# Feed-forward down products: seven products of quarters in place of eight, in all chunks but each stage's first, with the gated units' hidden tiles cut 6, 8, 8

## The reference, cut to what matters

```python
# two MLP stages, i = 0, 1 (D_FF = 4096)
u = jnp.square(jax.nn.relu(h @ mlp_w1[i])) @ mlp_w2[i]
h = _layer_norm(DN_ALPHA * h + u, ln2_g[i], ln2_b[i])
...
# four gated stages (D_FF_2 = 2816), layers l = 0, 1, before and after a mixer
def _swiglu(x, w_gate, w_up, w_down):
    return (jax.nn.silu(x @ w_gate) * (x @ w_up)) @ w_down
x = x + MACARON * _swiglu(_rmsnorm(x, ffn1_norm), ffn1_w_gate, ffn1_w_up, ffn1_w_down)
```

## Time and profile before

| | |
|---|---|
| device time, median of 3 runs | 3332.48 us (3332.04 to 3334.54) |
| span of the profiled execution, first to last instruction | 3327.9 us |
| outside the span, against the median | 4.6 us |
| PE busy | 3224.8 us, 97% |
| DVE busy | 2011.6 us, 60% |
| ACT busy | 1456.2 us, 44% |
| POOL busy | 872.9 us, 26% |

### The profile page before, as it was taken

One profiled execution on the slowest core, in us unless ns is written; L12 is line 12 of the kernel. 1 busy time (PEld: TensorE's weight loads), 2 busy tenths in 40 slices (PEclk: granted clock), 3 DMA queues, 4 the chain that ended last, 5 costly groups with the idle time before them and its releaser, 6 DMA issues.

```text
span 3327.9 us, 47776 instructions
## 1 busy us (share of the span) xinstructions
PE 3224.8 (97%) x20089; PEld 2867.4 (86%) x20092; DVE 2011.6 (60%) x3009; ACT 1456.2 (44%) x2244; POOL 872.9 (26%) x401
## 2 busy tenths in 40 slices
PE   8999999999999999999999999999999999999998
PEld 6887889988668899888999788999999998789998
DVE  6568755445866544576747636574766476367646
ACT  4465445443534544454434324453454343235433
POOL 3210033321400233303232430323222323312232
PEclk9999999999999999999999999999999999999999
DMA  4310233331102333323222322332332323223332
GB/s 133 105 50 26 99 98 112 101 119 58 64 26 89 102 114 102 109 71 125 92 85 97 114 81 84 115 102 83 115 102 89 103 83 125 76 89 108 96 96 76
DMA packets 239814, 308.97 MB, mean 93 GB/s; under 512 B 8336, under 2 KB 168096, under 8 KB 239088
## 3 DMA queue, kind: packets, MB, share of 16 engines
q1 hardware_dynamic: 236016, 291.41, 26.8%
q0 software_dynamic: 3584, 14.52, 1.2%
HBM read 303.80 MB, written 2.10 MB: 92 GB/s over the span
## 4 chain that ended last, share of the span: by engine, by line
PE 78%; DVE 16%; ACT 4%; issue 2%; DMA 0%; POOL 0%; DVEq 0%; ACTq 0%; POOLq 0%
PE bank L598 24%; PE bank L600 24%; PE bank L599 24%; DVE wlo L2082 3%; ACT whi L1322 2%; PE bank L979 1%; DVE wraw L2104 1%; DVE xl L2155 1%; PE bank L618 1%; DVE raw_w L2104 1%; PE bank L1261 1%; PE bank L1252 1%; PE bank L1186 0%; DVE st L2113 0%; DVE wkk_o L2899 0%
## 5 line engine op out<-in xcount | busy, mean ns | idle before, releaser
L3140 POOL TENSOR_TENSOR wlo<-wraw,whi 128x1024 fp32r<-128x1024 f32 (+2 forms) x209 | 531.1, 2545 | 1374.3 <-ACT whi L1322 1374.1
L598 PE MATMUL bank<-xh,whi 128*128 128x256 f32 (+1 forms) x2456 | 721.0, 294 | 46.4 <-DVE zt L2277 17.9
L1322 ACT ACTIVATE whi<-wraw 128x1024 fp32r<-128x1024 f32 (+3 forms) x426 | 441.1, 1039 | 678.7 <-PE bank L600 546.2
L600 PE MATMUL bank<-xh,wlo 128*128 128x256 f32 (+1 forms) x2456 | 715.7, 291 | 0.0
L599 PE MATMUL bank<-xl,whi 128*128 128x256 f32 (+1 forms) x2456 | 711.8, 290 | 0.0
L3140 POOL TENSOR_TENSOR wlo<-raw_w,whi 128x1024 fp32r<-128x1024 f32 (+1 forms) x126 | 300.6, 2389 | 867.4 <-ACT whi L1322 867.4
L598 PEld LDWEIGHTS bank<-xh,whi 128*128 128x128 f32 x2456 | 464.5, 189 | 66.8 <-issue 27.1
L598 PE MATMUL bank<-whi,uh_w 128*128 128x512 f32 x1216 | 473.9, 390 | 0.0
L600 PE MATMUL bank<-whi,ul_w 128*128 128x512 f32 x1216 | 473.3, 389 | 0.0
L599 PEld LDWEIGHTS bank<-xl,whi 128*128 128x128 f32 x2456 | 464.5, 189 | 10.2
L599 PE MATMUL bank<-wlo,uh_w 128*128 128x512 f32 x1216 | 473.2, 389 | 0.0
(11 more groups left out here) (392 smaller groups left out, 5009.7 us busy)
## 6 DMA issues: line engine op xcount, KB each, us to landing
wraw<-in_w_in SPq DMA_DIRECT2D x26, 1024.0 KB, 5.1
wraw<-in_ffn_w_down SPq DMA_DIRECT2D x20, 1024.0 KB, 5.0
raw_w<-in_ffn_w_down SPq DMA_DIRECT2D x20, 1024.0 KB, 5.1
raw_w<-in_mlp_w SPq DMA_DIRECT2D x19, 1024.0 KB, 5.1
wraw<-in_mlp_w SPq DMA_DIRECT2D x17, 1024.0 KB, 5.3
wraw<-in_ffn_w_gate SPq DMA_DIRECT2D x32, 512.0 KB, 4.6
raw_w<-in_ffn_w_gate SPq DMA_DIRECT2D x32, 512.0 KB, 4.8
raw_w<-in_ffn_w_up SPq DMA_DIRECT2D x32, 512.0 KB, 4.4
```

What stands on the lines that cost most here:

```text
L598: M.matmul(o, lh, rh, start=start, stop=False, skip_group_check=more)
L600: return M.matmul(o, ll, rh, start=False, stop=stop, skip_group_check=more)
L1322: A.activation(hi, raw, ACT.Copy).then_inc(*k.w_hi.inc(("hi", j)))
L3140: G.tensor_tensor(lo[:, 0:n], raw[:, 0:n], hi[:, 0:n].bitcast(F), ALU.subtract).then_inc(*k.w_lo.inc(("lo", j)))
```

## The change

The down product of every chunk but a stage's first is now done by the same scheme of seven products. The two operands are u (two halves of 256 tokens by two halves of 4 hidden tiles) and the down weights of the chunk (two halves of 4 hidden tiles by two halves of 512 columns). The planner's new `grid` writes 14 items for such a chunk (seven products, each in two parts of 2 hidden tiles, called a and b here, as in 5a and 5b); an item is now 2 token tiles x 2 hidden tiles x 3 = 12 matmuls of 128x512. The order of issue is 1, 2, 5, 6, 3, 7, 4.

- TensorE: 168 matmuls of 128x512 for a chunk in place of 192 (`grid` in the tensor program). Products 1, 6, 7 share one bank for each token tile, as do 5 and 3; a later product of such a chain adds to what stands in the bank, after VectorE has read it.
- ScalarE: 14 high parts of weights of 1024 columns (before 8), and the seven high parts of u's operands with 1024 columns (`u_high`) in place of eight with 512.
- VectorE: four sums of u quarters (`u_sum`, for 7, 6, 5 and 3), seven low parts of u's operands with 1024 columns (`u_low`) in place of eight with 512, eight sums of weight quarters (5, 6, 7 and 4, two parts each), three low parts of weights (3a, 3b, 4b; `ON_DVE`), and 16 additions of a bank to `h` (`add`) in place of 8.
- GpSimd: 11 low parts of weights (before 8).
- Gated stages are cut 6, 8, 8 (`GLU_PARTS`) instead of 8, 8, 6, so the chunk of 6 is the plain first one. All up units of a gated stage now have four tiles.
- The down weights arrive as four loads of 4 tiles x 512 columns, each filling a raw slot until the last of its products has been split.
- The load of `pT` stands in the MLP's first chunk instead of its last, into another buffer; the reserved DMA scratch is set to 8192 bytes.

The diff, cut to its core: the tables and the planner, TensorE's new `grid`, then the MLP's rows in the scalar program (`high_u`, `u_high`) and in the vector program (`u_sum`).

```diff
+GLU_PARTS = ((0, 6), (6, 14), (14, 22))
+GRID = (1, 2, 5, 6, 3, 7, 4)
+CHAIN = {1: "a", 6: "a", 7: "a", 5: "b", 3: "b", 2: "c", 4: "d"}
+HOST = {1: "11", 2: "21", 3: "22", 4: "21", 5: "11", 6: "11", 7: "12"}
+ADDS = {1: ((0, 0),), 2: ((0, 0),), 5: ((1, 1),), 6: ((0, 1),), 3: ((0, 1),), 7: ((1, 1), (1, 0)), 4: ((1, 0),)}
+ON_DVE = ((3, 0), (3, 1), (4, 1))
...
+    def grid(self, tag, key, view):
+
+        u, pair = Unit(key, 0, 0), self.pairs(4)
+        for n, (name, k, c) in enumerate((("11", 0, 0), ("21", 4, 0), ("12", 0, 512), ("22", 4, 512))):
+            u.loads[name] = self.load(view[:, k:k + 4, c:c + 512], [2 * pair[n], 2 * pair[n] + 1])
+            self.loads[u.loads[name]].name, self.loads[u.loads[name]].unit = name, u
+        for p in GRID:
+            u.items[p] = [self.item(tag, u.loads[HOST[p]], 1, 2 * part, 2 * part + 2, "dve" if (p, part) in ON_DVE else "pool", u, p, part)
+                          for part in range(2)]
...
+    def grid(u, last, turn_after):
+
+        tail = 0
+        for p in GRID:
+            key = [("grid", u.key, CHAIN[p], t) for t in range(2)]
+            uh, ul = k.wide.u[p]
+            for part in range(2):
+                j = slots.get("down")
+                wh, wl = weights(j)
+                pe.wait_ge(at("u operand", u.key, p))
+                for t in range(2):
+                    if part == 0 and p in (1, 5, 2, 4):
+                        take(key[t], True)
+                    elif part == 0:
+                        pe.wait_ge(at("added", u.key, {6: 1, 7: 6, 3: 5}[p], t))
...
+            def high_u(n, p):
+                if q and (n, p) in ((1, 1), (1, 5), (1, 4)):
+                    u_high(d, {1: 1, 5: 7, 4: 2}[p], at("u used", "up", i, q - 1))
...
+                u_high(d, 5, at("u used", "up", i, q - 1))
+                grid(d, last, 2, between=high_p if last else None)
...
+                u_sum(d, 6)
+                u_sum(d, 5)
+                grid(d, 1.0, last, 2, between=low_p if last else None)
```

More of the change, by code:

```diff
@@ L261, in load, with item @@
         return len(self.loads) - 1
-    def item(self, tag, load, n, k0, kn, low, unit=None, p=None):
+    def item(self, tag, load, n, k0, kn, low, unit=None, p=None, part=0):
         if n == 2:
@@ L268, in item @@
         before = sorted({self.split_at[x] for x in halves if x in self.split_at})
-        self.items.append(Item(tag, self.loads[load], halves, before, k0, kn, low, unit, p))
+        self.items.append(Item(tag, self.loads[load], halves, before, k0, kn, low, unit, p, part))
         for x in halves:
@@ L1036, in glu @@
         s = k.wide
-        parts = chunks(DFF2 // 128)
+        parts = GLU_PARTS
         g = 2 * l + which
@@ new lines, in u_low, with grid @@
+    def u_low(d, p):
+        hi, lo = k.wide.u[p]
+        dve.wait_ge(at("u high", d.key, p))
+        V.tensor_tensor(lo, k.wide.u32[p], hi.bitcast(F), ALU.subtract).then_inc(*done.inc(("u operand", d.key, p)))
+    def grid(u, scale_y, last, turn_after, stage=None, between=None):
+        tail = 0
+        for p in GRID:
+            for part in range(2):
+                slots.get("down")
+                slots.done()
+                if part == 0 and p in (1, 2, 5, 6):
+                    if p == 2:
+                        u_sum(u, 3)
+                    u_low(u, {1: 5, 2: 6, 5: 3, 6: 4}[p])
+                if part == 0 and p == 3 and between:
+                    between()
+                if part:
+                    add(u, p, scale_y, last, stage)
+                if last and p in (7, 4) and tail < 3:
+                    if tail == turn_after:
+                        ho.finish(1)
+                        ho.turn(0)
+                    if tail == min(turn_after + 1, 2):
+                        ho.turn(1)
+                    if tail >= turn_after:
+                        slots.prepare()
+                    tail += 1
@@ new lines, in add @@
+    def add(u, p, scale_y, last, stage):
+        for n, (th, ch) in enumerate(ADDS[p]):
+            for t in range(2):
+                tt, c, key = 2 * th + t, 512 * ch, ("grid", u.key, CHAIN[p], t)
+                x = h[:, tt, c:c + 512]
+                dve.wait_ge(at("product", u.key, p, t))
+                if p in (2, 3, 7, 4):
+                    dve.wait_ge(at("added to", u.key, {2: 1, 3: 6, 7: 5, 4: 7}[p], t) if n == 0 else None)
+                names = [("added to", u.key, p, t)]
+                if n == len(ADDS[p]) - 1:
+                    names.append(("added", u.key, p, t))
+                    if p in (2, 3, 7, 4):
+                        names.append(("free", key))
+                ends = last and ENDS.get(p) == (th, ch)
+                if ends:
+                    names.append(("h", ho.round, tt, c))
+                V.scalar_tensor_tensor(x, ring.of(key)[:, :], scale_y, x, ALU.mult, ALU.add).then_inc(*done.inc(*names))
+                if ends:
+                    if stage and p == 4 and t:
+                        barrier(stage)
+                    ho.updated(tt, c, p in (3, 4))
```

336 lines of the change are left out of this document (235 added, 101 removed).

## The result

The changed kernel takes 3492.66 us (median, 3490.93 to 3495.71), the kernel before 3332.26 in the same comparison: a ratio of 1.0481, 95% interval 1.0466 to 1.0496. It is 160 us slower. The forecast was 3442 with a range to 3495, so the sign and the range held, and the size was 51 us short. The result lies 2 us inside the range's upper end, and outside the stretch of 3400 to 3465 to which the prediction gave its best chance.

A forecast was written before the change was run, and what follows sets the result against it. TensorE's matmul count bounds the kernel now; in quarters, VectorE and GpSimd excluding each other on SBUF would. Six MLP chunks +55 and four gated stages +54, together +109 on 3332.5, gave 3442 us, range 3345 to 3495.

The forecast's parts named there:

- the lock: Down product in quarters: VectorE instructions with two SBUF inputs and GpSimd low parts exclude each other; 45.3 us against 38.3 of matmuls.
- walk: Queue-by-queue timing of a quarter down product: 52.9 us in an MLP, 50.5 in a gated stage, against 43.7 before.
- first mark 11.65: MLP down product: GpSimd has item 2b's low part ready at 11.65 us after TensorE's first matmul, due at 8.2.
- the handover at the end of a stage: Last down product of a stage (45.5 against 43.7 us): left as it is, bounds 0 and 2 us for each of six.
- locked instructions: VectorE instructions with both inputs in SBUF, which exclude a GpSimd low part for their whole length; taken at 1.18 us each.
- so it gives nothing back: Up product behind an MLP's quarter down product: 37.9 us of VectorE and GpSimd taking turns in 39.7, costed at no change.
- bound from above: Raw slots of down weights held until 7b is split at 42.7 us; queued loads cost 0 to 3 us a chunk, up to 40.
- a gain of under 1 us a stage: Gated stages' up units with four tiles instead of two: same matmuls, half the instructions per tile, costed at nothing.
- the forecast's span of 3437: Whole kernel: +109 us on the profile's own 3327.9 us; the same +109 on 3332.5 gives the forecast time 3442.
- the clock rival: TensorE's waits in quarter chunks also drop its clock, 1.7 us a fall, 24 or 48 us in all: 3466 to 3490, chance 0.15.
- 20 us fewer on GpSimd: Argument against the faster rival: up products run without a stall because they have 20 us fewer on GpSimd than quarter down products.
- The fast rival: Quarter down products: supply keeps up, stalls stay under 5.5 us a chunk; 3281, or 3256 with the remaining queue hidden; chance 0.13.

## Why the prediction was right in sign and short in size

**Right: the lock is the bound of a down product in quarters.** The walk's 52.9 and 50.5 us were 50.2 and 48.0, its first mark 11.65 was 11.56, its waits were ended by GpSimd's low parts, and the sums are lengthened to 3.4 us. In the run in which GpSimd only writes, the lock is gone and the sums fall to 1.22. In the middle MLP chunk there were five such waits and not seven, in the gated one seven.

**Missed, +37 us: the handover at the end of a stage.** This is the term of the sum that failed: the prediction left it as it is, because "its transposes are the same and its norms find TensorE waiting for VectorE anyway; bounds 0 and 2 us for each of six". With its walk the last chunks would have taken 54.7 us in an MLP (45.5 + 9.2), 52.3 in a gated stage and 50.5 in the final one; they took 62.9 and 61.9, 59.0 three times, and 52.5, 37 us more. (The run with plain last chunks won 95 us where the walk's 2 x 9.2 + 4 x 6.8 is 46: another 12 us lay in the up products ahead and in the stages behind.) VectorE in the last chunk of the first MLP, in the changed kernel:

```profile
735.04 2.20 DVE L2251 TENSOR_TENSOR raw_w<-raw_w 128x1024 f32<-128x1024 f32 x1
737.15 3.42 DVE L2916 TENSOR_TENSOR al_w<-zt,ah_w 128x1024 fp32r<-128x1024 f32 x1
740.49 3.42 DVE L2251 TENSOR_TENSOR raw_w<-raw_w 128x1024 f32<-128x1024 f32 x1
743.84 0.68 DVE L2496 SCALAR_TENSOR_TENSOR h<-bank,h 128x512 f32<-128x512 f32 x1
...
746.91 1.28 DVE L2285 SCALAR_TENSOR_TENSOR h<-h,rs,gb 128x1024 f32<-128x1024 f32 x1
...
752.40 3.38 DVE L2229 TENSOR_TENSOR wlo<-raw_w,whi 128x1024 fp32r<-128x1024 f32 x1
```

```profile
748.25 1.97 PE L655 MATMUL bank<-con,h 128*128 128x128 f32 x8 [2.35 <-DVE h L2285]
752.54 1.97 PE L655 MATMUL bank<-con,h 128*128 128x128 f32 x8 [2.32 <-DVE h L2285]
755.84 0.79 PE L635 MATMUL bank<-whi,uh_w 128*128 128x512 f32 x1 [1.33 <-DVE wlo L2229]
```

The last addition to a row block and its norm are 4.3 us of VectorE, and two of them stand in a row from 743.84 on, with 4b's low part behind. TensorE waits for each and then for the low part, 6 us in all. The kernel before makes the same norms at the same place: there too the first two row blocks are complete together, three items of TensorE ahead of their transposes, and TensorE does not wait for them. There, VectorE stood idle until the bank of the first row block was complete, 31.5 us into the chunk:

```profile
703.05 0.69 DVE L2293 SCALAR_TENSOR_TENSOR h<-bank,h 128x512 f32<-128x512 f32 x1 [5.04 <-PE bank L600]
```

In quarters TensorE was done with product 3, which completes the first two row blocks, at 734.65, and VectorE came to its first addition at 743.84, 9.2 us late: three locked instructions, drawn out to 2.2 and 3.4 us, stood ahead of it. In the gated chunk from 1857.8 on it is 5.9 us late, behind two. So the norms did not find TensorE waiting anyway; they found VectorE late.

That the backlog is the cause is read from the traces: no run puts product 3's additions ahead of the locked work. Two runs bear on it. Where GpSimd only writes, VectorE is late by 1.5 us in the first MLP's last chunk, yet this chunk still takes 50.7 us, with waits of 1.16 for the norm and 2.20 for 4b's low part behind it, so the amount of VectorE's work there costs time even without the lock. And the moved norm shows that its place against product 7's additions gives nothing.

Part of the +37 us is the clock. TensorE behind the first of these waits (columns as in the earlier trace rows):

```profile
748.30:761.30 13.00, 9.35 (x28) 6.88 (x28) 12.79 (x16) 6.22 (x10) 8.28 (x3) 0.50 0.35 112
```

This chunk is 12.7 us longer than a middle one: 6.0 are the three waits, 3.9 the transposes (1.97 us for eight, where the same group takes 1.09 at full clock in the run with the norm moved), and 2.7 are 4b's 12 matmuls, which take 5.5 us at the lower clock. So 4.5 of the 12.7 us are the clock. TensorE is busy for 48.6, 47.1, 45.7, 44.2, 44.1 and 44.0 us in the six last chunks; a middle one at a granted clock of 1.00 has 40.6, and 16 transposes add 2.1 to all but the final one. That is an estimate of 20 us at most for the six, part of it hidden by other waits. No run takes the clock and the waits apart.

**Missed, +40 us: the up product behind a quarter chunk.** The prediction costed it as "so it gives nothing back", from the lock alone (37.9 us in 39.7). Its own bound from above names the mechanism, raw slots held until 7b is split, "0 to 3 us a chunk, up to 40". It had been looked for in the down product and falls into the up product, and its size is 5 us in each of eight up products and not up to 3 in each of 14; that both come to 40 in all is luck. That late loads are the bulk of it is shown for the four up products of the MLPs, not for the gated ones. The price of the loads was taken from one load's 4.9 us; here eight are issued within 7.4 us.

**Over, -18 us:** the walk was 2.5 us too long in seven of the eight middle chunks, behind 7a.

**Missed, -8.5 us:** the cut to 6, 8, 8, "a gain of under 1 us a stage", gave 8.5 us of span and 10.5 of median by itself, 2 to 3 a stage. Then 37 + 40 - 18 - 8.5 is 50 of the 56 us between the forecast's span of 3437 and 3493; the other 6 are spread over the starts of stages.

**The range held by luck.** Its upper end of 3495 was put there for the clock rival, with a forecast of 3442 below it. What carried the time to 3493 was two other terms, +37 and +40, which two terms in the other direction, -18 and -8.5, brought back under it; only a part of the +37 is the clock. A slip that changed nothing: the up products do not have "20 us fewer on GpSimd" but 17 (26.4 - 9.6).

**The clock.** It fell, as the rival had it, at the wait for 2b. Two stretches of the middle MLP chunk at and behind that wait:

```profile
612.80:616.80 4.00, 0.84 (x2) 0.75 (x3) 4.00 (x2) 1.54 (x2) 3.33 (x2) 0.79 0.00 0
616.80:620.00 3.20, 3.20 (x9) 2.43 (x9) 2.06 (x4) 2.00 (x2) 3.20 (x2) 0.50 0.00 0
```

Behind 3.24 us of waiting the granted clock is 0.50, the 1.2 GHz level. This hardly lengthened the chunk, which ended 2.7 us ahead of a walk at full clock: TensorE still had 1.59 us to wait at 6b for the lock. In gated middles, where no wait is over 2.3 us, the clock stayed at 1.00. The length of one wait does not decide it: where GpSimd only writes, a wait of 3.29 us in the middle MLP chunk left it at 1.00, and in the changed kernel's gated last chunk it was 0.50 behind one of 2.33. The Trainium skill, "TensorE: Matmul & The Clock Gate", section "HAM oscillation — how this bites in real kernels", says that a matmul engine that keeps waiting falls back to half rate. The trace agrees for the MLPs' chunks and the last ones and not for the gated middles. The price was hidden in the middle MLP chunk and paid at the ends of stages (above), so the rival was right in part.

**The fast rival** (3256 to 3281) needed stalls under 5.5 us a chunk. Even without the lock and with plain last chunks the time is 3336, so the runs leave it no room: the up products lose 28 us, twice what the middles then gain.

## What to carry to other kernels

Before matmuls are traded for element-wise work, count the work of VectorE with two SBUF inputs and GpSimd's reads as one engine, per stretch and not over the span. Then ask for each stretch what it hands on: a chunk that holds all its buffers to the end starves the one behind it, and when VectorE's queue is late at a stage's end, so is the norm that the next stage waits for. When a stretch gets shorter in an experiment, look at the one behind it before believing it.

## What the runs showed of the hardware

- A memset on GpSimd does not hold the lock: in the run where it only writes, VectorE's sum at 610.33 took 1.22 us under a pair of memsets from 609.17 to 611.15.

```profile
610.33 1.22 DVE L2251 TENSOR_TENSOR wraw<-raw_w,wraw 128x1024 f32<-128x1024 f32 x1
```

```profile
609.17 1.98 POOL L3387 MEMSET wlo<- 128x1024 f32 x2
```

  The Trainium skill, "SBUF — State Buffer", section "Who interferes with whom", speaks of a GpSimd instruction that reads SBUF, and the trace agrees.
- Back to back, both engines' records come to the same 3.4 us, 2.2 of it waiting on VectorE and 1.0 on GpSimd, so neither's busy time is its own work. GpSimd shows 27.0 us in a chunk for ten low parts, 2.70 each against 2.40 alone.
